# A two-block transformer kernel: the expert front in one stage, selected tables and gelu blocks in another order, and gates and norms of the second block's mixers rewritten

## What is computed

```python
def _peer(x, wq, keys, u, v):        # 8 heads, 128 x 128 experts, top 16
    q = (hb @ wq).reshape(tc, PEER_HEADS, 2, PEER_HALF)
    s = jnp.einsum('thpk,hpnk->thpn', q, keys)
    s_top, i_top = lax.top_k(s, PEER_TOPK)
    ...
    act = jax.nn.gelu(jnp.einsum('td,thed->the', hb, u[eid]), approximate=False)
    return jnp.einsum('the,thed->td', g * act, v[eid])

def gated_deltanet(q, k, v, z, b, a, conv_w, a_log, dt_bias, norm_g):
    ...
    beta = gate_chunks(jax.nn.sigmoid(b))
    g = -jnp.exp(a_log) * jax.nn.softplus(a + dt_bias)
    ...
    o = rmsnorm(from_chunks(o), norm_g)
    o = o * jax.nn.silu(z)           # hgrn2 ends in the same way: rmsnorm(o) * silu(g)
```

## Time and profile before

| | |
|---|---|
| median of 3 runs | 4238.05 us (4232.57 to 4238.93) |
| profiled execution | 4234.1 us |
| its span, granted clock | 4232.3 us, 0.967 |
| PE busy | 3958.9 us, 94% |
| PEld busy | 3541.9 us, 84% |
| DVE busy | 3054.3 us, 72% |
| ACT busy | 1828.5 us, 43% |
| DMA | 755.32 MB, mean 178 GB/s |

### The profile page before, as it was taken

How to read it: one execution, slowest core, us unless ns; L and a number is a source line. 1 busy time by engine, 2 the same in 40 slices (tenths; PEclk the granted TensorE clock), 3 DMA queues, 4 the chain that set the end, 5 groups by cost and what they waited for, 6 DMA issues and landing times. The chain is left out here.

```text
span 4232.3 us, 66491 instructions
## 1 busy us (share of the span) xinstructions
PE 3958.9 (94%) x25970; PEld 3541.9 (84%) x25970; DVE 3054.3 (72%) x6862; ACT 1828.5 (43%) x2893; POOL 5.8 (0%) x16
## 2 busy tenths in 40 slices
PE   7997999999998999999989899999999688997899
PEld 5766999988888989978868799998888677987798
DVE  3556696778886867778975569677888667765776
ACT  3343444433334444433434344444333544555364
POOL 0000000000000000000000000000000000000000
PEclk8998999999999999999989999999999899998999
DMA  5142575556666865567651347555676321442143
GB/s 209 65 162 105 173 233 166 174 183 242 239 233 236 318 227 167 171 226 255 239 183 65 124 144 234 175 174 174 243 249 240 130 104 59 188 167 91 55 177 143
DMA packets 122981, 755.32 MB, mean 178 GB/s; under 512 B 15856, under 2 KB 17392, under 8 KB 58288
## 3 DMA queue, kind: packets, MB, share of 16 engines
q1 hardware_dynamic: 122672, 751.08, 50.7%
HBM read 695.45 MB, written 55.57 MB: 177 GB/s over the span
## 5 line engine op out<-in xcount | busy, mean ns | idle before, releaser
L1847 DVE TENSOR_TENSOR expert_ring_low<-expert_ring,expert_high 128x1024 fp32r<-128x1024 f32 x768 | 935.9, 1220 | 266.0 <-ACT expert_high L2060 265.5
L2060 ACT ACTIVATE expert_high<-expert_ring 128x1024 fp32r<-128x1024 f32 x768 | 811.2, 1057 | 654.0 <-PE ps L2011 653.1
L1979 PE MATMUL ps<-peer_hT_high_peer,expert_high 128*128 128x256 f32 x3072 | 887.0, 289 | 10.0 <-DVE expert_ring_low L1847 9.6
L1981 PE MATMUL ps<-peer_hT_high_peer,expert_ring_low 128*128 128x256 f32 x3072 | 865.4, 282 | 0.0
L1980 PE MATMUL ps<-peer_hT_low,expert_high 128*128 128x256 f32 x3072 | 865.4, 282 | 0.0
L1979 PEld LDWEIGHTS ps<-peer_hT_high_peer,expert_high 128*128 128x128 f32 x3072 | 588.4, 192 | 12.6 <-DVE expert_ring_low L1847 11.7
L1980 PEld LDWEIGHTS ps<-peer_hT_low,expert_high 128*128 128x128 f32 x3072 | 589.0, 192 | 0.0
L1981 PEld LDWEIGHTS ps<-peer_hT_high_peer,expert_ring_low 128*128 128x128 f32 x3072 | 583.8, 190 | 0.0
L2011 PE MATMUL ps<-expert_high,weighted_high 128*128 128x512 f32 x1536 | 477.0, 392 | 25.3 <-DVE weighted_low L1874 25.3
L2011 PE MATMUL ps<-expert_ring_low,weighted_high 128*128 128x512 f32 x1536 | 475.4, 391 | 0.0
L2011 PE MATMUL ps<-expert_high,weighted_low 128*128 128x512 f32 x1536 | 475.1, 391 | 0.0
(11 more groups left out here) (641 smaller groups left out, 7106.3 us busy)
## 6 DMA issues: line engine op xcount, KB each, us to landing
expert_ring<-in_peer_u SPq DMA_DIRECT2D x192, 1024.0 KB, 5.3
expert_ring<-in_peer_v SPq DMA_DIRECT2D x192, 1024.0 KB, 4.9
gelu_peer<-gelu_out SPq DMA_DIRECT2D x192, 256.0 KB, 5.5
gelu_in_peer<-gelu_peer SPq DMA_DIRECT2D x96, 512.0 KB, 5.7
weight_ring<-in_ffn_w_up SPq DMA_DIRECT2D x22, 2048.0 KB, 7.3
weight_ring<-in_w_in SPq DMA_DIRECT2D x14, 2048.0 KB, 7.5
weight_ring<-in_w_mod SPq DMA_DIRECT2D x12, 2048.0 KB, 7.4
weight_ring<-in_peer_wq SPq DMA_DIRECT2D x12, 2048.0 KB, 7.2
```

What stands on the lines that cost most here:

```text
L1847: dve.tensor_tensor(piece(low, n), piece(raw, n), high[:, n % LEAD, :].bitcast(F32), ALU.subtract).then_inc(low_done, 1)
L1979: pe.matmul(o, b[:, s], hT_h[:, c, :], start=(c == 0), stop=False)
L1981: mm = pe.matmul(o, lo[:, s], hT_h[:, c, :], start=False, stop=(c == DC - 1))
L2060: act.activation(high[:, n % LEAD, :], piece(raw, n), ACT.Identity).then_inc(high_done, 1)
```

## The change

**Front.** A new stage `peer_queries` holds transposes and projection. TensorE turns chunks 0 to 3 first and the others two by two between the quarters of unit 0, whose four output blocks grow side by side in banks 0 to 3; ACT and DVE take a quarter of the weights and a pair of chunks in turn. SP issues the moves, the weights' run-ahead, and the first pieces of the expert ring as soon as the weight slot beneath them is released.

```diff
+def peer_queries(nc, G, u0, tiles, col, hs, whole, pq, moves, src_u):
...
+            for c in range(4):
+                turn(c)
+            for i, u in enumerate(units):
...
+                if i == 0:
+                    for q in range(QUARTERS):
+                        if q < 2:
+                            turn(4 + 2 * q)
+                            turn(5 + 2 * q)
+                        pe.wait_ge(low_done, q + 1)
+                        pe.wait_ge(hs_low, 2 * q + 2)
+                        for n in own:
+                            for c in (2 * q, 2 * q + 1):
+                                products(n, c)
...
+            for q in range(QUARTERS):
+                c = 2 * q + 1
+                part(0, q)
+                act.wait_ge(turned, c + 1)
...
+                act.activation(whole[:, c % WHOLE, :], ps[:, 4 + c % 4, 0:W], ACT.Identity, scale=scale(c),
+                               bias=shift(c)).then_inc(s_whole, 1)
+                for k, sem in ((c - 1, v_whole), (c, s_whole)):
+                    act.wait_ge(sem, q + 1)
+                    act.activation(high[:, k, :], whole[:, k % WHOLE, :], ACT.Identity).then_inc(hs_high, 1)
...
+            ws.run_ahead(sp)
+            slots = sorted((max(u for u in units if u % SLOTS == s), s) for s in range(E_SLOTS // 2))
+            for u, s in slots:
+                sp.wait_ge(*ws.release[u])
+                for k in (2 * s, 2 * s + 1):
+                    sp.dma_start(G.e_raw[:, k, :], src_u[k]).then_inc(G.e_landed[k], 16)
```

```diff
+        def expert(p):
+            return (p + N_KEYS - KEPT) % N_KEYS
...
-                at["sel"] = at["now"]
                 for t in range(PT):
+                    at[f"turn{t}"] = at["now"] + TURN_AFTER
+                    yield (TURN_AFTER + 1) * SELECT_NS
                     dve.wait_ge(sel_turned, t + 1)
...
-                dve.tensor_tensor(aw[:, :], ge_in[:, m % 2, r % 4, :], wt[:, r, :], ALU.mult).then_inc(aw_done, 1)
+                ge = ge_out[:, r, :] if r < KEPT else ge_in[:, m % 2, r % 4, :]
+                dve.tensor_tensor(aw[:, :], ge, wt[:, expert(r), :], ALU.mult).then_inc(aw_done, 1)
...
+            for n in range(SCORES // 2):
+                dve.wait_ge(score_ready, 2 * n + 1)
+                dve.tensor_copy(*scores_of(2 * n)).then_inc(score_v, 1)
+                if n < LEAD:
+                    split_low(n)
...
+            for g in range(SCORES):
...
+                for n in range(n0, n0 + 4):
+                    mm = pe.matmul(ps[:, 4 + g % 4, (n - n0) * P:(n - n0 + 1) * P], pq[:, n, t * P:(t + 1) * P], keysT[:, n, :],
+                                   start=True, stop=True)
+                mm.then_inc(score_ready, 1)
...
+                if r == N_KEYS - 1:
+                    table_out(GROUPS - 2)
+                    table_out(GROUPS - 1)
                 split_high(r + LEAD)
```

```diff
-        yield T
-        act.wait_ge(S.consts_landed, B.consts)
+        yield 21.8
         act.activation(B.ea[:, :], B.row[:, 0, :], ACT.Exp).then_inc(S.act_step, 1)
+        yield T + 0.3
...
-        act.activation(B.ba[:, :, :], B.small[:, :, 64:68], ACT.Sigmoid).then_inc(S.act_step, 1)
-        yield T + 0.6
+        act.activation(B.ba[:, :, :], B.small[:, :, 64:68], ACT.Exp, scale=-1.0).then_inc(S.act_step, 1)
...
-    GATES = 46.0
+    GATES = 42.2
...
+            act.wait_ge(*((S.first_ready, 1), (S.second_ready, 1))[t])
+            for h in range(4):
+                last = act.activation(B.sq[:, t, h, :], self.bank((4, 7)[t])[:, h, :], ACT.Square, accum_out=B.dn_ms[:, t, h, 0:1])
...
+            step(dve.reciprocal(B.dn_ms[:, t, :, 0], B.dn_ms[:, t, :, 1]))
+            step.wait()
+            step(dve.tensor_tensor(dst, self.bank((4, 7)[t]), B.dn_ms[:, t, :, 0:1].broadcast_to([P, 4, P]), ALU.mult))
+            step.wait()
+            dve.wait_ge(S.gained, 4)
+            step(dve.tensor_tensor(dst, dst, B.sz[:, t, :].rearrange("p (h c) -> p h c", h=4), ALU.mult))
```

More of the change, by code:

```diff
@@ L1660 @@
 DEAD_FROM = 48
-ROWS_AT = 50
-HELD_FROM = 56
+ROWS_AT = 54
+HELD_FROM = 60
 HELD_NS = 300
+KEPT = 4
+TURN_AFTER = 2
 class Arena:
@@ L1700, in top16, with peer_experts @@
     step.wait()
-def peer_experts(nc, G, hs, scores, arena, dead, wt, small, src_u, src_v, ge_dram, back, mod, end):
+def peer_experts(nc, G, hs, queries, scores, arena, dead, wt, small, src_u, src_v, ge_dram, back, mod, end):
     ps = G.ps
@@ L1843, in select @@
                     yield 600
+                assert at[f"turn{PT - 1}"] < TABLE_AT
             def split_low(n):
@@ L2278, in peer @@
         ws.limit = None
-        peer_experts(nc, G, hs, scores, later, dead, wt, (table, hot_i, hot_j, ge_in, aw, ah, G.w_low), src_u, src_v, ge_dram,
+        peer_experts(nc, G, hs, (pq, keysT), scores, later, dead, wt, (table, hot_i, hot_j, ge_in, aw, ah, G.w_low), src_u, src_v, ge_dram,
                      [(G.x[:, ts, :], G.x_spill[:, ts, :])], mod, end)
@@ L3299, in out_act, with gains @@
         act.activation(B.wkT[:, :, :], self.bank(5), ACT.Identity).then_inc(S.wkT_out, 1)
-        yield T + 5.0
-        act.wait_ge(S.dn_ms_ready, 1)
-        act.activation(B.dn_ms[:, 0, :, 1], B.dn_ms[:, 0, :, 0], ACT.Sqrt).then_inc(S.dn_rms_ready, 1)
-        yield T + 9.0
-        act.wait_ge(S.dn_ms_ready, 2)
-        act.activation(B.dn_ms[:, 1, :, 1], B.dn_ms[:, 1, :, 0], ACT.Sqrt).then_inc(S.dn_rms_ready, 1)
+        for t in range(2):
+            yield T + (2.4, 7.2)[t]
+            act.wait_ge(*((S.first_ready, 1), (S.second_ready, 1))[t])
+            for h in range(4):
+                last = act.activation(B.sq[:, t, h, :], self.bank((4, 7)[t])[:, h, :], ACT.Square, accum_out=B.dn_ms[:, t, h, 0:1])
+            last.then_inc(S.dn_ms_ready, 1)
+            act.wait_ge(S.dn_ms_ready, t + 1)
+            act.activation(B.dn_ms[:, t, :, 1], B.dn_ms[:, t, :, 0], ACT.Sqrt, scale=1.0 / DN_DHEAD,
+                           bias=B.eps[:, 0:1]).then_inc(S.dn_rms_ready, 1)
+    def gains(self, dve):
+        S, B = self.S, self.B
+        yield 117.0
+        dve.wait_ge(S.s_out, self.in2.total["s"])
+        dve.wait_ge(S.norms_landed, 32)
+        for t in range(2):
+            dve.tensor_tensor(B.sz[:, t, :], B.sz[:, t, :], B.wdn[:, :], ALU.mult).then_inc(S.gained, 1)
+            yield 118.5 + 3 * t
+            dve.tensor_tensor(B.cg[:, t, :], B.cg[:, t, :], B.whg[:, :], ALU.mult).then_inc(S.gained, 1)
+            yield 120.0
     def out(self, dve):
@@ L3311, in out @@
         dve.tensor_copy(B.u[:, :, :], self.bank(3)).then_inc(S.first_out, 1)
-        step(dve.tensor_copy(B.o[:, 0, :, :], self.bank(4)))
         yield T + 3.0
@@ L3770, in norm_act @@
-        act.activation(B.hg_ms[:, :, :, 1], B.hg_ms[:, :, :, 0], ACT.Sqrt).then_inc(S.hg_rms_ready, 1)
+        for t in range(2):
+            yield self.SCAN + 4.6 + 3.8 * t
+            act.wait_ge(S.hgo_ready, t + 1)
+            for h in range(4):
+                last = act.activation(self.by_head(B.hg_sq[:, t, :])[:, h, :], self.by_head(self.o(t))[:, h, :], ACT.Square,
+                                      accum_out=B.hg_ms[:, t, h, 0:1])
+            last.then_inc(S.hg_ms_ready, 1)
+            act.wait_ge(S.hg_ms_ready, t + 1)
+            act.activation(B.hg_ms[:, t, :, 1], B.hg_ms[:, t, :, 0], ACT.Sqrt, scale=1.0 / HG_DHEAD,
+                           bias=B.eps[:, 0:1]).then_inc(S.hg_rms_ready, 1)
@@ L3895, in mixer_2 @@
             B.state = late.take("hg_state", [P, 4, 2, P], F32)
-            B.oc = late.take("hg_o", [P, 2, SEQ], F32)
             B.ex = late.take("hg_decays", [P, 2, 3 * P], F32)
@@ L3957, in _ @@
                           delta.norm(dve), delta.decays(dve), delta.qk_out(dve), delta.pairs(dve), delta.solve(dve),
-                          delta.out(dve), sparse.index(dve), sparse.attend(dve), hgrn.forget(dve), hgrn.after(dve),
+                          delta.gains(dve), delta.out(dve), sparse.index(dve), sparse.attend(dve), hgrn.forget(dve), hgrn.after(dve),
                           hgrn.prepare(dve), hgrn.scan(dve), hgrn.norm(dve))
```

309 lines of the change are left out of this document (182 added, 127 removed).

## The result

The changed kernel takes 4122.97 us (median of 4 runs, 4108.15 to 4124.32) where the kernel before takes 4238.49 (4 runs, 4232.57 to 4244.96): a ratio of 0.9719, with a 95% interval of 0.9693 to 0.9746. Profiled run: 4121.8 us, span 4120.1, clock 0.978. One of the four runs is 14 to 16 us shorter than the others; its trace was not kept, and a stretch of 24 us at the lower clock that is there in some executions and not in others (experiment 11) is worth 10 to 12 us.

The account below looks back on a forecast made before the run. It took gapless TensorE work as the bound, with gains only at the joints between stretches: fronts 26.5, selected table 18.0, U to V 19.6, mixers 27.8, sum 91.9 us off the 4238 median, giving 4146, range 4128 to 4180.

Parts of the forecast that it names:

- part D: Second block's mixers, twice: shorter waits at gates and end, 13.9 us each, 27.8 us in all.
- A, front: Three expert fronts, first transpose to first gelu: barriers and old order go, saving 9.7, 6.9 and 9.9, together 26.5 us.
- Rival 1: Fronts give less: waits between quarters and full score banks cost 18 us, giving 4164 us; chance 0.13.
- B, selected table: Transposes of the selected table, three times: moved later, they no longer wait; 18.0 us saved, 13.8 of it waits.
- C, V start: From U to V, three times: rotated order leaves a 1.9 us wait in place of 8.4, saving 19.6 us.
- the clock is taken to fall all the same: At the first V products: slow products still follow the remaining 1.9 us wait, so no clock gain was counted.
- D, gates: Second block's mixer gates: fewer table loads before the squares save 6.8 us; the hoisted Exp costs 1.1, a silu load returns 1.2.
- End: Each second-block mixer's end: squares with sums on ACT shorten the closing vector chain, 7.5 us less, 0.5 lost to early gains.
- Rival 3: Clock stays up over the short gaps ahead of the V products: 9 us more gain, 4137 us; chance 0.10.
- Rivals 2, 4 and 5: Mixers absorb their gain, 4164 (0.12); query projection stays at 1.2 GHz, 4264 (0.03); V wait stays, 4166 (0.04).
- The drain (rival 6): At the mixers' gates, each table switch also costs a drain: 2 x 3.35 us more gain, 4139 us; chance 0.02.

Follow-up runs that it names:

- experiment 11: The changed kernel run again twice, with nothing altered, for more times and profiles; the first repeat took 4122.05 us, ratio 0.9733 to the kernel before.
- experiment 3: The kernel before with only the two times of Hgrn.after moved (TURN + 5.4 and + 6.8): 4228.2 us, ratio 0.9972.
- experiment 5: The changed kernel with the old gates of the second block's mixers put back: 4133.6 us, ratio 0.9746 to the kernel before.
- experiments 7 and 8: Changed kernel, first with unit 0's query blocks filled one by one (4124.4 us, 0.9731), then with the V loop's old order (4131.6 us, 0.9755).
- experiment 10: The kernel before with unused identity products ahead of the first V product: 60 of them gave ratio 1.0013, 32 gave 0.9982 (4229.4 us).

## Why the prediction was wrong

The step that failed is part D of the sum, the second block's mixers: 27.8 forecast, 44.9 measured. It put at nothing a wait that the change removes, the 4.05 us for silu_z in each mixer: 8.1 us of idle time, 11.7 with the clock by experiment 3. With it the forecast would have been 4134 and the range, moved by as much, 4116 to 4168, with 4123 inside. The rest is size: the direction and mechanism of the terms that the sum had were right, its parts were 29 us short together, and it was luck that 10 us went the other way, in code that nobody touched; without them the time would lie 15 us below the range and not 5.

- **A, front: mechanism right, term under.** 61.4, 61.8 and 61.4 us against 62.0, 64.0 and 62.4. The second front's stall was 0.9 to 1.5, not 2, and its products started at 1.00, where I had charged 15 slow ones. Rival 1 (stalls of 6 us a front) did not come: the 1.9 us are one wait a front ahead of its first product, and between the quarters there is none.
- **B, selected table: right.** Idle 13.6 against 13.8; the clock's part 7.6 in all in place of my 4.2.
- **C, V start: right in the wait** (1.94 against 1.9 reckoned, 19.5 us of idle time against 19.6), **wrong in "the clock is taken to fall all the same"**. Behind 1.94 us it stayed up in the first PEER and fell for 3.4 us in the other two: 4.5 us less than before. Neither side of this was sure: the ten profiles without fillers at stage ends that have this wait have it 30 times, and the clock fell behind 14.
- **D, gates: right in sum** (13.5 by experiment 5, 13.8 forecast), though the wait itself came out at 2.1 and not 3.4. **End: right** (7.1 each against 7.0; its chain adds up to 3541.55 and not 3541.7, which changes nothing). **Missed: Hgrn's two times.** The prediction names neither the two shifted yields nor the wait across which they reorder ACT. It stood in the list of waits of before as "PE ps L3446 <- ACT silu_z", 8.1 us in two, and the rows left it out.
- **The clock.** I counted slow products behind the waits I looked at, one by one, and none in C and D. Measured less idle time, the clock's part is 9.0 us in A, 7.6 in B, 4.6 in C and 5.8 in D. In the first mixer's 132 us it was 0.93 before and is 1.00 after: it fell three times there, the last time in the gap at the end, and now not once, although a wait of 1.6 us (L3377, now L3540) with a fall behind it before is still there. Rival 3, at 10%, had 9 us of this in C; half of it came.
- **Rivals 2, 4 and 5** did not come: the mixers kept all of theirs, the fronts ran at 0.95, 1.00 and 0.96, and no DMA releases the first V products.
- **The drain (rival 6)** did not come: a load and the operation behind it are 1.29 us apart, and the undone gates bring the 10.2 us waits back with six switches of 1.55. The page "ScalarE: Activation LUTs" of the Trainium skill (What ACT_TABLE_LOAD costs) gives 2.66 us for a switch with its drain; no trace here shows that.
- **Range.** It was built for shortfalls (4180) and took only 18 us on the other side. The clock's recovery had been left out of C and D and put low in B; these errors have one sign and add up.

## What to carry to other kernels

Go through the profile's list of waits from the top and ask of each whether any line of the diff moves an instruction in front of it; a shift of one microsecond in a table of times can be worth more than a rewritten function. Price a removed wait as wait plus the slow products behind it, as a range: behind the same 1.94 us wait the clock fell in about half of the cases. Compare stretches of traces as well as medians: three of the effects here, of 12 to 15 us each, don't show in the medians, where a stretch elsewhere comes and goes. Before filling a wait with unused work, measure one filler in the trace: twice the assumed length turned a gain of 9 us (4113) into a loss of 27 (4149).

## What the hardware showed that was not expected

TensorE's clock can fall while the engine is busy without a gap: 23.9 us at 0.50 in the window 2167.40 of the changed kernel, right behind 10 us at 1.00, where the kernel before is at 1.00. Two idle stretches of 11.5 and 7.9 us lie shortly ahead of it; in the three profiles in which the first was filled it wasn't there. In four of the seven other unfilled profiles the clock falls in the same code without a gap too, for 3.4 us in experiments 7 and 8 and for 6.8 in both tries of experiment 10. Whether the long stretch comes goes with a few tenths of a us in the time of an earlier fall (experiment 11). A matmul of two plain 32-bit 128x128 tiles is two records and 0.22 us, a transpose through the identity 0.12 (1.94 us for 16 at full speed in the second front before).
